# Expert gate and up weights in halves of the contraction, and the shared expert's down products in the last octets, in a two-layer hybrid model with mixture-of-experts

## The reference

```
h = layer_norm(ALPHA * h + mixer(h) @ w_out)
h = layer_norm(ALPHA * h + moe(h))
```

```
scores = sigmoid(x @ router_w)                      # 64 experts in 8 groups
4 groups, then 8 experts per token, chosen by scores + router_bias
wts = 2.5 * scores[chosen] / sum(scores[chosen])
routed = sum over the chosen e of wts[e] * (silu(x @ w_gate[e]) * (x @ w_up[e])) @ w_down[e]
shared = (silu(x @ sw_gate) * (x @ sw_up)) @ sw_down
moe(x) = routed + shared
```

## Time and profile before

| | |
|---|---|
| median of the runs | 1270.3 us |
| the profiled execution's own time | 1272.9 us |
| its span | 1271.2 us |
| TensorE busy | 1167.8 us, 92% |
| DVE, ScalarE, POOL busy | 38%, 15%, 4% |
| moved by DMA | 463.8 MB, mean 365 GB/s |
| TensorE's granted clock, mean | 0.996 |

### The profile page before, as it was taken

One profiled execution on the slowest core, in us unless ns is written; L12 is line 12 of the kernel. 1 busy time (PEld: TensorE's weight loads), 2 busy tenths in 40 slices (PEclk: granted clock), 3 DMA queues, 4 the chain that ended last, 5 costly groups with the idle time before them and its releaser, 6 DMA issues.

```text
span 1271.2 us, 17795 instructions
## 1 busy us (share of the span) xinstructions
PE 1167.8 (92%) x7237; PEld 569.4 (45%) x7237; DVE 486.9 (38%) x1053; ACT 193.4 (15%) x330; POOL 46.7 (4%) x76
## 2 busy tenths in 40 slices
PE   9999999988889888888899999999888998888886
PEld 7774743433333333332387657333333333333332
DVE  5894633333323222322237255332223233322224
ACT  3231211111111111110122312111111111111102
POOL 6200100000000000000010001000000000000000
PEclk9999999999999999999999999999999999999999
DMA  9775969999999999999953277999999999999993
GB/s 345 200 297 191 421 264 421 421 420 421 421 420 423 422 421 421 423 419 421 401 177 135 103 291 312 369 420 421 420 422 421 421 422 421 422 422 421 421 421 137
DMA packets 76125, 463.78 MB, mean 365 GB/s; under 512 B 8544, under 2 KB 9888, under 8 KB 25376
## 3 DMA queue, kind: packets, MB, share of 16 engines
q1 hardware_dynamic: 75920, 462.37, 89.5%
q10 hardware_dynamic: 144, 0.52, 0.1%
HBM read 456.51 MB, written 6.36 MB: 364 GB/s over the span
## 4 chain that ended last, share of the span: by engine, by line
DMA 47%; PE 46%; SPq 3%; DVE 2%; issue 1%; ACT 1%; DVEq 0%
DMA expert_weights<-in_exp_w_up 43%; PE bank L1115 21%; PE bank L646 4%; PE bank L1150 3%; PE bank L632 3%; PE bank L720 2%; PE bank L736 2%; SPq L303 2%; DMA weight_ring<-in_sh_w_down 2%; PE bank L993 1%; DMA expert_weights<-s_rows 1%; PE bank L747 1%; PE bank L1081 1%; PE bank L1070 1%; PE bank L1042 1%
## 5 line engine op out<-in xcount | busy, mean ns | idle before, releaser
L1115 PE MATMUL bank<-expert_weights,weight_ring 128*64 128x512 f32 x1536 | 342.8, 594 | 34.3 <-DMA expert_weights<-in_exp_w_up 34.3
L1150 PE MATMUL bank<-expert_weights,hiddenT 128*32 128x512 f32 x2048 | 233.0, 595 | 15.7 <-ACT weight_ring L1362 8.5
L1115 PEld LDWEIGHTS bank<-expert_weights,weight_ring 128*64 128x64 f32 x1536 | 123.9, 137 | 246.2 <-issue 245.9
L1968 DVE TENSOR_TENSOR hidden<-silu_gate,bank 128x256 f32<-128x256 f32 x64 | 27.0, 421 | 439.2 <-ACT silu_gate L1371 439.2
L1115 PE MATMUL bank<-expert_weights,hT 128*64 128x512 f32 x512 | 120.3, 612 | 40.2 <-DMA expert_weights<-in_exp_w_up 40.2
L1150 PEld LDWEIGHTS bank<-expert_weights,hiddenT 128*32 128x32 f32 x2048 | 60.7, 109 | 143.0 <-issue 117.7
L1371 ACT ACTIVATE silu_gate<-bank 128x256 f32<-128x256 f32 x64 | 24.6, 385 | 486.0 <-PE bank L1115 486.0
L1115 PEld LDWEIGHTS bank<-expert_weights,hT 128*64 128x64 f32 x512 | 40.2, 139 | 120.6 <-issue 120.6
L1978 DVE TENSOR_SCALAR y_top<-bank,slot_gate 128x512 fp32r<-128x512 f32 x64 | 48.1, 751 | 97.5 <-PE bank L1150 97.5
L1375 ACT ACTIVATE y_top<-bank,slot_gate 128x512 fp32r<-128x512 f32 x64 | 44.0, 688 | 254.6 <-PE bank L1150 254.6
L1985 DVE SCALAR_TENSOR_TENSOR y_low<-bank,slot_gate,y_top 128x512 fp32r<-128x512 f32 x64 | 48.1, 751 | 57.6 <-ACT y_top L1375 57.6
(11 more groups left out here) (375 smaller groups left out, 982.6 us busy)
## 6 DMA issues: line engine op xcount, KB each, us to landing
expert_weights<-in_exp_w_gate SPq DMA_DIRECT2D x128, 1024.0 KB, 15.0
expert_weights<-in_exp_w_up SPq DMA_DIRECT2D x128, 1024.0 KB, 17.1
expert_weights<-in_exp_w_down SPq DMA_DIRECT2D x128, 1024.0 KB, 19.0
weight_ring<-in_w_in_even SPq DMA_DIRECT2D x5, 2048.0 KB, 10.1
weight_ring<-in_w_out SPq DMA_DIRECT2D x4, 2048.0 KB, 7.9
weight_ring<-in_w_in_odd SPq DMA_DIRECT2D x4, 2048.0 KB, 10.4
s_c<-expert_weights SPq DMA_DIRECT2D x1, 3072.0 KB, 9.8
expert_weights<-s_c SPq DMA_DIRECT2D x1, 3072.0 KB, 10.4
```

The costliest lines, as they stand in the source:

```text
L1115: last_mm = nc.tensor.matmul(bank[6][a * 2 * CAP:(a + 1) * 2 * CAP, :].rearrange("p (w f) -> p w f", w=2), octet_tokens(l, v, c)[:, 2 * q ...
L1150: last_mm = nc.tensor.matmul(bank[b][by_tile:by_tile + CAP, :], hm[:, j, own:own + CAP], ew_d(2 * u + a)[:, j, half * 512:(half + 1) * 512 ...
L1968: nc.vector.tensor_tensor(hslot[:, :], sg[:, :], bank[6][:, DE:2 * DE], ALU.mult)\
```

## The change

1. Gate and up weights are loaded by halves of the contraction (chunks 0 to 3 and 4 to 7): four DMAs of 0.5 MB per expert with rows of 4 KB, on the semaphores `gu_in` and `gu_rest`. The gate and up product waits for the second halves only before chunk 4. In the opening pair `gu_half` is raised after chunk 3, and the first refill's first halves are issued on it. The last pair's down weights are loaded by halves of the columns (rows of 2 KB).
2. The eight shared down products leave the opening: four (j = 0) go one each into pairs 24 to 27, four (j = 1) in twos into pairs 28 and 29. In their place, four products of a zero one-hot with a zero `y_top` open the accumulation in banks 0 to 3. The wait for the `sh_d` weights stays. The four ALPHA*h products leave `scatter_last`: one each in pairs 28 and 29, two in pair 30. They read a copy of the scaled identity that POOL makes. For this the shared hidden values and half of the gathered tokens move to other places in SBUF, and the shared gate and up products to banks 4 and 5.
3. The two rank products stand after three of the eight chunks of the last `shared_up`. On DVE the selection of the first octet comes before the shared hidden values and before the load of `npass`; the selection for a next pass is made in the last pair, with two clearings.
4. The second half of `dve_s5_inputs` in mixer 0 moves behind L1533 to L1544.

```diff
+        def expert_half(sp, l, e, s, part, landed):
+            lo, hi = part * EW // 2, (part + 1) * EW // 2
             src_g = A["exp_w_gate"][l, e].rearrange("(p c) f -> p (c f)", c=KC)
             src_u = A["exp_w_up"][l, e].rearrange("(p c) f -> p (c f)", c=KC)
-            sp.dma_start(ew[:, s, 0:EW], src_g).then_inc(m["gu_in"][s], 16)
-            sp.dma_start(ew[:, s, EW:2 * EW], src_u).then_inc(m["gu_in"][s], 16)
+            sp.dma_start(ew[:, s, lo:hi], src_g[:, lo:hi]).then_inc(landed, 16)
+            sp.dma_start(ew[:, s, EW + lo:EW + hi], src_u[:, lo:hi]).then_inc(landed, 16)
...
-            expert_load(sp, m, l, s, s)
-            sp.dma_start(ew[:, s, 2 * EW:3 * EW], down_src(l, s)).then_inc(m["d_in"][s], 16)
+            expert_half(sp, l, s, s, 0, m["gu_in"][s // 2])
+            expert_half(sp, l, s, s, 1, m["gu_rest"][s // 2])
+            sp.dma_start(ew[:, s, 2 * EW:3 * EW], down_src(l, s)).then_inc(m["d_in"][s // 2], 16)
...
+            def refill(base, it, u):
+                sp.wait_ge(m["gu_full"], (base - 1) * 2 + u + 1)
+                for part, landed in ((0, m["gu_in"]), (1, m["gu_rest"])):
                     for s in (2 * u, 2 * u + 1):
-                        expert_load(sp, m, l, it * NSLOT + s, s)
-                    sp.wait_ge(m["y_hi_full"], (base - 1) * 2 + u + 1)
-                    for s in (2 * u, 2 * u + 1):
-                        sp.dma_start(ew[:, s, 2 * EW:3 * EW], down_src(l, it * NSLOT + s)).then_inc(m["d_in"][s], 16)
-            with sp.Fori(1, NE // NSLOT) as it:
-                group(it, it)
...
+            def first_refill(ps):
+                sp.wait_ge(m["gu_half"], ps + 1)
+                for s in range(2):
+                    expert_half(sp, l, NSLOT + s, s, 0, m["gu_in"][0])
+                sp.wait_ge(m["gu_full"], ps * PAIRS + 1)
+                for s in range(2):
+                    expert_half(sp, l, NSLOT + s, s, 1, m["gu_rest"][0])
+                sp.wait_ge(m["y_hi_full"], ps * PAIRS + 1)
+                for s in range(2):
+                    sp.dma_start(ew[:, s, 2 * EW:3 * EW], down_src(l, NSLOT + s)).then_inc(m["d_in"][0], 16)
+            def last_refill(ps):
+                sp.wait_ge(m["gu_full"], ps * PAIRS + PAIRS - 2)
+                for part, landed in ((0, m["gu_in"]), (1, m["gu_rest"])):
+                    for s in (2, 3):
+                        expert_half(sp, l, NE - NSLOT + s, s, part, landed[1])
+                sp.wait_ge(m["y_hi_full"], ps * PAIRS + PAIRS - 2)
+                for s in (2, 3):
+                    down_half(sp, l, NE - NSLOT + s, s, 0, m["d_in"][1])
+                for s in (2, 3):
+                    down_half(sp, l, NE - NSLOT + s, s, 1, m["d_rest"])
+            def refills(ps):
+                first_refill(ps)
+                refill(ps * (NE // NSLOT) + 1, 1, 1)
+                with sp.Fori(2, NE // NSLOT - 1) as it:
+                    for u in range(2):
+                        refill(ps * (NE // NSLOT) + it, it, u)
+                refill(ps * (NE // NSLOT) + NE // NSLOT - 1, NE // NSLOT - 1, 0)
+                last_refill(ps)
...
+            nc.gpsimd.tensor_copy(alpha_once, alpha[:, :]).then_inc(S["alpha_once"], 1)
...
-            shared_up(1, 0, P, SEQ).then_inc(m["sh_gu"], 1)
-            shared_up(1, 1, 0, SEQ).then_inc(m["sh_gu"], 1)
+            shared_up(1, 0, P, SEQ)
+            shared_up(1, 1, 0, SEQ, range(3))
             pe.wait_ge(m["chosen"], 1)
             both = chosen[:, :, :].rearrange("p t e -> p (t e)")
             nc.tensor.matmul(bank[7][:, 0:TT * NE], upper[:, :], both, start=True, stop=True)
             nc.tensor.matmul(bank[7][0:1, TT * NE:2 * TT * NE], ones[:, 0:1], both, start=True, stop=True)\
               .then_inc(m["rank_psum"], 1)
+            shared_up(1, 1, 0, SEQ, range(3, KC)).then_inc(m["sh_gu"], 1)
...
             def scatter_last(par):
+                pe.wait_ge(m["y_parts"], npass * PAIRS + 1)
                 for t in range(TT):
-                    for n in range(2):
-                        nc.tensor.matmul(bank[2 * t + n][:, :], alpha[:, :], h[:, t, n * 512:(n + 1) * 512],
-                                         start=False, stop=False, skip_group_check=True)
-                    if t == 0:
-                        pe.wait_ge(m["y_parts"], npass * PAIRS + 1)
...
+            def add_alpha_h(t, n):
+                nc.tensor.matmul(bank[2 * t + n][:, :], alpha_once, h[:, t, n * 512:(n + 1) * 512],
+                                 start=False, stop=False, skip_group_check=True)
...
+            def shared_down(j, t, n):
+                nc.tensor.matmul(bank[2 * t + n][:, :], shid[:, j, t * P:(t + 1) * P], wd[:, j, n * 512:(n + 1) * 512],
+                                 start=False, stop=False, skip_group_check=True)
             ring_arrived(pe, f"sh_d{l}")
             wd = slot_of(f"sh_d{l}")[:, 0:JE * D].rearrange("p (j n) -> p j n", j=JE)
-            shared_down(0)
-            shared_down(1).then_inc(S["shared_done"], 1)
+            pe.wait_ge(m["pt_ready"], 1)
+            pe.wait_ge(m["y_parts"], 1)
+            for t in range(TT):
+                for n in range(2):
+                    nc.tensor.matmul(bank[2 * t + n][:, :], onehotT[slot_rows(t), 1, :],
+                                     y_top[slot_rows(t), n * 512:(n + 1) * 512], start=True, stop=False,
+                                     skip_group_check=True)
+            pe.wait_ge(S["alpha_once"], l + 1)
             pe.wait_ge(m["low_part"], TT)
             pe.wait_ge(m["npass"], 1)
             npass = pe.value_load(npass_i[0:1, 0:1], min_val=1, max_val=MAX_PASS)
...
-                            pe.wait_ge(m["gu_in"][2 * u + a], 32 * g + 32)
+                        pe.wait_ge(m["gu_in"][u], 64 * g + 64)
                         for c in range(KC):
                             if opening:
                                 pe.wait_ge(m["xg_hi" if c % 2 else "xg_lo"], n + c // 2 + 1)
+                            if c == KC // 2:
+                                pe.wait_ge(m["gu_rest"][u], 64 * g + 64)
                             for a in range(2):
                                 last_mm = nc.tensor.matmul(
                                     bank[6][a * 2 * CAP:(a + 1) * 2 * CAP, :].rearrange("p (w f) -> p w f", w=2),
                                     octet_tokens(l, v, c)[:, 2 * q + a, :, :].rearrange("p t s -> p (t s)"),
                                     ew_gu(2 * u + a, c), start=(c == 0), stop=(c == KC - 1))
+                            if opening and c == KC // 2 - 1:
+                                last_mm.then_inc(m["gu_half"], 1)
                         last_mm.then_inc(m["gu_full"], 1)
...
+                        if last and v == 0:
+                            shared_down(0, q // 2, q % 2)
+                        if ending and q < 2:
+                            shared_down(1, q, 0)
+                            shared_down(1, q, 1)
+                            add_alpha_h(q, 0)
+                        if ending and q == 2:
+                            add_alpha_h(0, 1)
+                            add_alpha_h(1, 1)
                         pe.wait_ge(m["ht_ready"], n + 1)
-                        for a in range(2):
-                            pe.wait_ge(m["d_in"][2 * u + a], 16 * g + 16)
+                        pe.wait_ge(m["d_in"][u], 32 * g + 32)
                         for half, b, free, full in ((0, 4, "xg_lo", "y_lo_full"), (1, 5, "xg_hi", "y_hi_full")):
                             if not ending:
                                 pe.wait_ge(m[free], n + 5)
+                            if ending and q == 3 and half:
+                                pe.wait_ge(m["d_rest"], 32 * ps + 32)
...
+                pe.wait_ge(m["sh_silu"], 1)
                 for c in range(KC):
+                    if c == 2:
+                        pe.wait_ge(m["sh_hidden"], 1)
...
-            dve_s5_inputs(dve, chain)
+            dve_s5_inputs(dve, chain, 0)
...
+            dve_s5_inputs(dve, chain, 1)
...
+            dve.wait_ge(m["sh_gu"], 2)
+            nc.vector.tensor_tensor(shid[:, :, :], sh_silu[:, :, :], bank[5][:, :].rearrange("p (j t) -> p j t", j=JE),
+                                    ALU.mult).then_inc(m["sh_hidden"], 1)
...
-            shared_hidden(dve, l, 0)
-            shared_hidden(dve, l, 1)
...
+            def next_pass(ps):
+                nc.vector.tensor_scalar(rank[:, :, :], rank[:, :, :], float(CAP), None, ALU.subtract)\
+                  .then_inc(m["rank_next"], 1)
+                nc.vector.memset(shid[:, :, :], 0.0)
+                nc.vector.memset(alpha_once, 0.0)
+                dve.wait_ge(m["rank_next"], ps + 1)
+                select(0)
+                weigh(0, 0, (ps + 1) * (NE // OCT) + 1)
...
-                        if not (ending and q == 3):
+                        if ending and q == 3:
+                            next_pass(ps)
...
+            select(0)
+            weigh(0, 0, 1)
```

(3 more changed lines are left out.)

93 lines of the change are left out of this document (42 added, 51 removed).

## The result

The changed kernel took 1275.4 us (median of 8 runs, 1273.8 to 1277.3), against 1270.3 us before (8 runs, 1269.9 to 1272.2) on the same chip: ratio 1.0039, 95% interval 1.0028 to 1.0050. It is 0.4% slower, where 1254.8 us (1249 to 1264) was predicted. The profiled execution took 1277.3 us (span 1275.6), 4.4 us of span more than before.

A forecast was written before the change was run, and what follows sets the result against it. The load rate was taken to bound the loop. Gains 1.7 + 6.75 + 0.9 + 6.75 + 4.4 = 20.5, less 5, gave 15.5 us: 1272.9 to 1257.4 profiled, median 1254.8 us, range 1249 to 1264.

The forecast's parts named there:

- The stream itself: Expert loads in both MoE loops: 4 KB rows at about 419 GB/s cost 0.083 us per pair, 5 us in all.
- the halves cost what the gain is: Rival on the load stream: 4 KB rows settle at some 409 GB/s, costing 19.2 us, time 1269; chance 0.05.
- the point at which the kernel turns slower: Rival on gate and up loads: below 408 GB/s the 20.5 us gain is lost; 1291 at 395; chance 0.05.
- Start of the stream: First refill of each layer issued 8.85 us earlier, less a new 2.1 us hole: net 6.75 us per layer.
- the hole of 2.1: New DMA idle of 2.1 us before pair 3's refill, which still waits for all of pair 1's product.
- Opening, layer 0: Start of layer 0's MoE loop: first gate and up product 5.3 us earlier, ends 3 and 6.1 us.
- Opening, layer 1: Start of layer 1's MoE loop: zero products replace the shared down products, also gaining 5.3 us.
- This wait stays: Layer 1's opening: the wait for the shared down weights remains, ahead of the four zero products, with no cost counted.
- Layer 0's tail: End of layer 0: the load of s_c limits the gain to 0.9 us instead of 3.75.
- Shared products and ALPHA*h in the loop: Products moved into pairs 24 to 30: hidden under the loads, cost nothing; uncovered 10.7 us per layer.
- Mixer 0: TensorE's idle for gate_cols goes as half of the S5 inputs on DVE moves behind: gain 1.7 us.
- Layer 1's tail: End of layer 1: halved last product saves 3.55 us and removed ALPHA*h products 0.85: gain 4.4 us.

The follow-up runs named there:

- e1: Kernel before, only the refills' gate and up weights in two halves with 4 KB rows, 0.5 MB a transfer; products wait for all: 1294.3 us, ratio 1.018.
- e2: Kernel before with refills in 4 KB row halves, each transfer taking both experts of a pair, 1 MB, six per pair: 1289.8 us, ratio 1.015.
- e4: Changed kernel with gate and up loads whole again (8 KB rows, 1 MB), all else of the change kept: 1258.0 us, ratio 0.990.
- e10: e9 with pair 3's refill also by halves, its first halves issued after half of pair 1's product: 1253.6 us, ratio 0.986.
- e5: Changed kernel with only pairs 2 and 31 loaded by halves, all other gate and up loads whole: 1255.9 us, ratio 0.988.
- e13: Changed kernel with loads and products halved by matrix, gates first, then ups, whole 8 KB row loads, experts alternating: 1258.7 us, ratio 0.991.
- e14: e13 plus s_c ahead of u1, the sh_d wait moved to its first read, and pair 3's refill in two steps: 1252.5 us, ratio 0.985.
- e8: Changed kernel with TensorE's wait for sh_d moved from the opening to ahead of the last octets: 1273.7 us, ratio 1.0017.
- e7: Changed kernel with the s_c load issued ahead of u1 at the layer change: 1272.9 us, ratio 1.001.
- e9: e5 with s_c issued ahead of u1 and pair 30 loaded by halves as well: 1255.1 us, ratio 0.988.
- e3: Kernel before with refills' gate and up loads halved by partitions, 0.5 MB transfers with 8 KB rows into 64 partitions: 2066 us.
- e11: Changed kernel with loads and products halved by expert, one expert's products then the other's, 8 KB rows: 1523.9 us, ratio 1.199.

## Why the prediction was wrong

- **The stream itself: the step that failed.** "I take 0.083" us per pair, from 419 GB/s. Measured 0.29 per pair (15.2 against 14.9), 17.4 us in the two layers instead of 5: the rate of a long run of 4 KB rows is 409 GB/s and not 419. The row behind it was 3 us of another load, and the step itself said so. The rival "the halves cost what the gain is" named the mechanism, the rate (409) and the price (0.32, 19.2 us) and got a chance of 0.05. e1, e2 and e4 show it with and without the rest of the change. Its time, 1269, was 6 us short, and it put the point at which the kernel turns slower below 408 GB/s, because the other gains were counted at 20.5 us; they came to 13 (17.4 less the 4.4 by which the span grew).
- **Start of the stream: mis-sized.** The first refill came 9.6 us earlier beyond mixer 0 (8.85 forecast), but the stream behind it lost 4.7 and 4.4 us (13.4 and 13.1 less 8.7), where the hole of 2.1 was forecast. Of the hole 0.5 and 0.8 us are there; e10's expectation, "some 2 us without a transfer", misread it too. The rest is slow packets behind the refill, which the prediction did not have, and a later last increment. An earlier first refill is worth little in any form: against e4 the last weights of layer 0 land 0.7 us earlier in e5, and 0.9 and 2.0 us later in e13 and e14, all of which start 3.4 to 3.7 us earlier.
- **Opening, layer 0: right**, 6.0 us beyond mixer 0 (forecast 5.3): the zero products took 0.74 us (1.0 taken), both `npass` loads were hidden.
- **Opening, layer 1: wrong.** 2.9 us relative to the start of the shared up products instead of 5.3. "This wait stays" was costed at nothing; it came to 1.43 us, and the lowered clock followed (e8 takes both away). SP issued sh_d at 763.44 us instead of 759.41, behind 15 instead of 9 expert transfers and an issue that held it for 4.7 us.
- **Layer 0's tail: the mechanism right** (s_c at 18 us behind the landing, so only 0.9 of 3.75 us), the sign wrong: +0.7 us, because the idle TensorE came back at the lower clock, 2.15 us for 1.20. e7 takes 3.5 us of wait away.
- **Shared products and ALPHA*h in the loop: right, but barely**: pairs 29 to 31 keep the loads' step, 15.1 to 15.4 us, with 0.2 us of waiting or none left in pairs 29 and 30. With whole loads in the loop TensorE becomes the bound of pairs 30 and 31 once these are halved (e9).
- **Mixer 0: right**, 2.1 us (1.7). **Layer 1's tail: right**, 4.7 us (4.4).

The misses in the opening of layer 1 (2.4 us), in the tail of layer 0 (1.6) and behind the first refills (some 5) would still have left a faster kernel. The term that turned the sign is the stream's, 12.4 us over its forecast, and e4 takes it away.

## What to carry to other kernels

When the loop is bound by the rate of its loads, take the price of a new row size from a long full-rate run of such rows, not from 3 us of another load: a 1% in rate here is 9 us over the two streams, more than the 7.1 that the split gave back. A load can be split along a boundary that leaves its rows whole (by matrix, not by contraction) without losing rate, as long as the products still alternate between the experts. But no form of the split was shown to beat whole loads here: e4 0.990, e5 0.988, e13 0.991, with overlapping intervals. Look first whether TensorE is ahead where the split is to help (e5, e9). A load that is late behind a stage (s_c, sh_d) is worth as much as the last product in front of it: order the queue by who waits first (e7, e8).

## What was not expected of the hardware

- 8 KB rows 421 to 422 GB/s, 4 KB rows 409 over a long run (worked out above from 413 for the mix), though 3 us of them stood at 419.
- Gate and up transfers into 64 partitions: 226 GB/s with the engines full (e3).
- Thirty-two records on 64 columns: 7.1 us alternating, 12.3 us one expert behind the other (e11).
- The 16 increments of one landing drift apart in a long stream: those of a single transfer lie within 0.4 us at 186 us and over 3.8 us at 621 us in the kernel before.
- The DMA engines read as full at 336 to 371 GB/s behind an early refill with 4 KB rows (changed kernel, and e5 at 165 us, below). With 8 KB rows, e13 is back at 428 GB/s between 180 and 185 us, behind a longer hole.

```profile
165.00:170.00 5.00, 4.79 (x42) 1.67 (x42) 2.72 (x6) 1.06 (x2) 0.00 (x0) 1.00 1.01 371
```
